# Two-block transformer kernel in fp32: the last four weight units of two projections used tile by tile

## The reference

```python
h = modulate(rms_norm(x, norm_g[0]), sh_m, sc_m)
y = stick_breaking_mixer(h, w_qkv, w_o)      # ends in o @ w_o, 1024 x 1024
x = x + gt_m * rms_norm(y, norm_g[1])
h = modulate(rms_norm(x, norm_g[2]), sh_f, sc_f)
g, u = split(h @ w_in)                       # 1024 x 5632
y = (silu(g) * u) @ w_out                    # 2816 x 1024
x = x + gt_f * rms_norm(y, norm_g[3])
```

## Time and profile before

| | |
|---|---|
| time, median of 3 | 2371.11 us (2367.22 to 2376.46) |
| the profiled execution, its own time | 2365.49 us |
| its span, first to last instruction | 2363.7 us |
| busy PE, PEld, DVE, ACT, POOL | 1796.4, 1117.7, 1291.7, 868.9, 904.2 us |
| mean granted clock of PE | 0.83 |

### The profile page before, as it was taken

How to read it: one execution, slowest core, us unless ns; L and a number is a source line. 1 busy time by engine, 2 the same in 40 slices (tenths; PEclk the granted TensorE clock), 3 DMA queues, 4 the chain that set the end, 5 groups by cost and what they waited for, 6 DMA issues and landing times. The chain is left out here.

```text
span 2363.7 us, 25240 instructions
## 1 busy us (share of the span) xinstructions
PE 1796.4 (76%) x8848; PEld 1117.7 (47%) x8848; DVE 1291.7 (55%) x2801; ACT 868.9 (37%) x2355; POOL 904.2 (38%) x699
## 2 busy tenths in 40 slices
PE   8898899868777787564443468885377897999998
PEld 6775676445435255110000014331055676888786
DVE  4633668877787665656767676566403623333201
ACT  3122344333444343233643353333225734222212
POOL 1300334374663444344555544445400122444343
PEclk9999888777788889786555679986579998999999
DMA  6111999999999999999999999999953011122121
GB/s 246 54 63 49 403 410 392 418 377 411 411 401 418 418 418 417 417 404 406 419 420 420 419 405 419 418 397 419 420 178 110 1 72 71 72 107 107 72 107 54
DMA packets 108494, 687.78 MB, mean 291 GB/s; under 512 B 12240, under 2 KB 13264, under 8 KB 40144
## 3 DMA queue, kind: packets, MB, share of 16 engines
q0 software_dynamic: 73728, 536.90, 55.3%
q1 hardware_dynamic: 34640, 149.27, 16.9%
HBM read 681.40 MB, written 2.10 MB: 289 GB/s over the span
## 5 line engine op out<-in xcount | busy, mean ns | idle before, releaser
L747 PE MATMUL ps<-arena 128*32 128x512 f32 (+5 forms) x4376 | 872.7, 587 | 377.0 <-ACT arena L1452 337.3
L1696 POOL DMA_INDIRECT arena<-in_experts,arena_u x512 | 608.6, 1189 | 770.9 <-PE ps L747 678.2
L2001 DVE CUSTOM_DVE_ANT_0 arena<-arena 128x1024 f32<-128x1024 f32 x512 | 653.2, 1281 | 384.3 <-DMA arena<-in_experts,arena_u 367.5
L747 PEld LDWEIGHTS ps<-arena 128*128 128x128 f32 (+2 forms) x4376 | 443.2, 167 | 735.5 <-ACT arena L1452 496.6
L1448 ACT ACTIVATE sel<-sel 128x1 f32<-128x1 f32 x512 | 102.8, 201 | 705.4 <-DVE sel L2001 697.7
L1717 POOL TENSOR_TENSOR r_low<-middle,r_low 128x1024 fp32r<-128x1024 f32 x74 | 178.7, 2415 | 463.5 <-ACT r_low L1533 463.5
L747 PE MATMUL ps<-r_low 128*128 128x512 f32 x1248 | 286.4, 391 | 5.3 <-DVE r_low L2059 3.8
L747 PEld LDWEIGHTS ps<-r_low 128*128 128x128 f32 x1248 | 234.6, 189 | 56.8 <-DVE r_low L2059 4.4
L1452 ACT ACTIVATE arena<-arena,sel 128x32 f32<-128x32 f32 x512 | 164.5, 321 | 16.8 <-ACT sel L1448 0.2
L1533 ACT ACTIVATE r_low<-middle 128x1024 fp32r<-128x1024 f32 x74 | 78.3, 1058 | 208.1 <-PE ps L747 208.1
L747 PE MATMUL ps<-upper,arena 128*128 128x384 f32 (+5 forms) x640 | 144.9, 412 | 3.2 <-issue 3.0
(11 more groups left out here) (203 smaller groups left out, 1721.2 us busy)
## 6 DMA issues: line engine op xcount, KB each, us to landing
arena<-in_w_front SPq DMA_DIRECT2D x88, 512.0 KB, 3.5
middle<-in_w_late SPq DMA_DIRECT2D x18, 2048.0 KB, 8.2
arena<-in_w_qkv SPq DMA_DIRECT2D x48, 512.0 KB, 10.7
gtrow<-in_w_ada SPq DMA_DIRECT2D x32, 512.0 KB
arena<-in_experts,arena_u POOLq DMA_INDIRECT x512
arena<-in_w_ada SPq DMA_DIRECT2D x16, 512.0 KB, 10.0
x<-in_x SPq DMA_DIRECT2D x4, 512.0 KB, 8.7
arena<-in_sub_keys SPq DMA_DIRECT2D x2, 1024.0 KB, 10.4
```

Source lines behind the costliest of these rows:

```text
L747: return nc.tensor.matmul(out_, lhsT, rhs, start=start, stop=stop_, skip_group_check=skip)
L1696: nc.gpsimd.indirect_dma_start(ring[n % RING], None, a["experts"], bass.IndirectOffsetOnAxis(ap=idxq[:, i % 4, k:k + 1], axis=0),).then_in ...
L2001: nc.vector.tensor_tensor_reduce(r[:, 0:D], r[:, 0:D], xrep[k % 4], 1.0, 0.0, ALU.mult, ALU.add, dots[:, n % 8:n % 8 + 1]).then_inc(s["dot ...
```

## The change

Three things are changed in what each engine does.

- **Two groups of four units.** Units 4 to 7 and units 70 to 73 go through `split_last`: PE first waits for all four units' `u_lo`, then goes over the token tiles, and for each tile issues the 24 matmuls of the four units. `y` is told after each tile. The four units need four buffers: units 4 to 7 have buffers of their own in a region that the attention has left, units 70 and 71 keep the two of before, units 72 and 73 stand where `a_lo` was. `split_after` says how many units must have been used before ACT may write a unit: none for 4 to 7, 3 and 4 for units 8 and 9, 52 for units 72 and 73, and u-1 for all others (70 and 71 too). ACT splits the units in the same order as before, except that unit 9 now comes right after unit 8.
- **Transposes and modulation per tile.** After tile t's branch, PE transposes its own tile into that tile's two banks; tile 0's transposes stand between the matmuls of tiles 2 and 3, the others behind tile 3. ACT modulates a tile in eight instructions of 128 x 128 (four for tiles 2 and 3, where DVE does the other four), then copies the tile to `a_hi` in one instruction of 128 x 1024; DVE subtracts it in one. Unit 8 waits once for all four tiles of `a_lo`.
- **Places.** `tail` and `tail_sq` have a place of their own for k = 0, since the first tiles' tails now run while `a_hi` is still read. The attention's two swap semaphores (`qswap`, `kswap`) become one, `swap`, with the sum of the counts.

The diff, cut to its core:

```diff
-        u_hi = [low3(32 + 8 * n, KD, P) for n in range(2)]
-        u_lo = [low3(36 + 8 * n, KD, P) for n in range(2)]
+        u_hi = [low3(32 + 8 * (u % 2), KD, P) for u in range(UNITS)]
+        u_lo = [low3(36 + 8 * (u % 2), KD, P) for u in range(UNITS)]
+        for n, kb in enumerate((112, 120, 84, 92)):
+            u_hi[UNIT_O2 + 4 + n], u_lo[UNIT_O2 + 4 + n] = high3(kb, KD, P), high3(kb + 4, KD, P)
+        for n in range(2):
+            u_hi[UNITS - 2 + n], u_lo[UNITS - 2 + n] = low3(16 + 8 * n, KD, P), low3(20 + 8 * n, KD, P)
+        def split_after(u):
+            if UNIT_O2 + 4 <= u < UNIT_FIN:
+                return 0
+            if UNIT_FIN <= u < UNIT_FIN + 2:
+                return UNIT_O2 + 3 + u - UNIT_FIN
+            return UNIT_FOUT if u >= UNITS - 2 else u - 1
...
-        tail_sq, tail_sq2 = region(8, D), region(120, D)
+        tail_sq, tail_sq2 = [region(kb, D) for kb in (104, 8)], region(108, D)
...
             def split_tile(out_, u, k, rows_hi, rows_lo):
                 for kd in range(KD):
-                    if u == UNIT_FIN:
-                        pe.wait_ge(s["a_lo"], kd + 1)
-                    mm(out_, u_hi[u % 2][:, kd, :], rows_hi[:, kd, :], kd == 0, False)
-                    mm(out_, u_hi[u % 2][:, kd, :], rows_lo[:, kd, :], False, False)
-                    ins = mm(out_, u_lo[u % 2][:, kd, :], rows_hi[:, kd, :], False, kd == KD - 1)
+                    if u == UNIT_FIN and kd == 0:
+                        pe.wait_ge(s["a_lo"], T)
+                    mm(out_, u_hi[u][:, kd, :], rows_hi[:, kd, :], kd == 0, False)
+                    mm(out_, u_hi[u][:, kd, :], rows_lo[:, kd, :], False, False)
+                    ins = mm(out_, u_lo[u][:, kd, :], rows_hi[:, kd, :], False, kd == KD - 1)
                 return ins.then_inc(s["unit_used"], 1)
-            def split_rows(out_of, u, k_of, cols_hi, cols_lo, kts, first, last):
-
-
-                w_hi, w_lo = halves(u_hi[u % 2]), halves(u_lo[u % 2])
+            def split_tile_rows(t, u, k_of, cols_hi, cols_lo, last):
+                w_hi, w_lo = halves(u_hi[u]), halves(u_lo[u])
+                tok = slice(t * P, (t + 1) * P)
+                for hf in range(2):
+                    kt, n = k_of(u, hf)
+                    out_ = ps[:, 2 * t + n, :]
+                    mm(out_, cols_hi[:, kt, tok], w_hi[:, hf, :], kt == 0, False)
+                    mm(out_, cols_hi[:, kt, tok], w_lo[:, hf, :], False, False)
+                    ins = mm(out_, cols_lo[:, kt, tok], w_hi[:, hf, :], False, kt == last)
+                return ins
+            def split_rows(units, k_of, cols_hi, cols_lo, last):
+                for u in units:
+                    unit(u)
+                    for t in range(T):
+                        ins = split_tile_rows(t, u, k_of, cols_hi, cols_lo, last)
+                    ins.then_inc(s["unit_used"], 1)
+            def split_last(units, k_of, cols_hi, cols_lo, last, between):
+                for u in units:
+                    unit(u)
                 for t in range(T):
-                    tok = slice(t * P, (t + 1) * P)
-                    for hf in range(2):
-                        kt, n = k_of(hf)
-                        begin, end = kt == first, kt == last
-                        mm(out_of(t, n), cols_hi[:, kt, tok], w_hi[:, hf, :], begin, False)
-                        mm(out_of(t, n), cols_hi[:, kt, tok], w_lo[:, hf, :], False, False)
-                        ins = mm(out_of(t, n), cols_lo[:, kt, tok], w_hi[:, hf, :], False, end)
-                    if t < T - 1 and end and kts is not None:
-                        ins.then_inc(s[kts], 1)
-                return ins.then_inc(s["unit_used"], 1)
+                    for u in units:
+                        ins = split_tile_rows(t, u, k_of, cols_hi, cols_lo, last)
+                    if t < T - 1:
+                        ins.then_inc(s["y"], 1)
+                    between(t)
+                ins.then_inc(s["unit_used"], len(units))
+                pe.wait_ge(s["unit_used"], units[-1] + 1)
+                nc.tensor.nop().then_inc(s["y"], 1)
...
-            for t in range(T):
+            def rows_after(t):
+                pe.wait_ge(s["yfree"], t + 1)
                 pe.wait_ge(s["xs"], T + t + 1)
                 for kd in range(KD):
-                    ins = mm(ps[:, kd, t * P:(t + 1) * P], x[:, t, kd * P:(kd + 1) * P], tdiag[:, t, :])
+                    ins = mm(ps[:, 2 * t + kd // 4, kd % 4 * P:(kd % 4 + 1) * P], x[:, t, kd * P:(kd + 1) * P], tdiag[:, t, :])
                 ins.then_inc(s["tr"], 1)
+            def o_rows(u, hf):
+                return (u - UNIT_O2) % 4 * 2 + hf, (u - UNIT_O2) // 4
+            split_rows(range(UNIT_O2, UNIT_O2 + 4), o_rows, a_hi, a_lo, KD - 1)
+            split_last(range(UNIT_O2 + 4, UNIT_FIN), o_rows, a_hi, a_lo, KD - 1, lambda t: rows_after(0) if t == 2 else None)
+            for t in range(1, T):
+                rows_after(t)
             for j in range(FT):
                 if j >= 4:
                     pe.wait_ge(s["ffd"], j - 3)
@@ -1276,12 +1308,11 @@
                     unit(UNIT_FIN + 2 * j + n)
                     split_tile(ps[:, 2 * j % 8 + n, :], UNIT_FIN + 2 * j + n, 1, a_hi, a_lo)
             pe.wait_ge(s["ffd"], FT)
-            for kt in range(FT):
-                unit(UNIT_FOUT + kt)
-                split_rows(lambda t, n: ps[:, 2 * t + n, :], UNIT_FOUT + kt, lambda hf: (kt, hf),
-                           act_hi, act_lo, "y", 0, FT - 1)
-            pe.wait_ge(s["unit_used"], UNITS)
-            nc.tensor.nop().then_inc(s["y"], 1)
+            def fout_rows(u, hf):
+                return u - UNIT_FOUT, hf
+            split_rows(range(UNIT_FOUT, UNITS - 4), fout_rows, act_hi, act_lo, FT - 1)
+            split_last(range(UNITS - 4, UNITS), fout_rows, act_hi, act_lo, FT - 1, lambda t: None)
...
-                if u >= 2:
-                    sc.wait_ge(s["unit_used"], u - 1)
-                nc.scalar.activation(u_hi[u % 2], raw_unit(u), ACT.Copy).then_inc(s["u_hi"], 1)
-
-            def high(kd):
-
-                sc.wait_ge(s["a_y"], KD * T + kd + 1)
-                nc.scalar.activation(a_hi[:, kd, :], y_hT[:, kd, :], ACT.Copy).then_inc(s["a_hi"], 1)
+                if split_after(u) > 0:
+                    sc.wait_ge(s["unit_used"], split_after(u))
+                nc.scalar.activation(u_hi[u], raw_unit(u), ACT.Copy).then_inc(s["u_hi"], 1)
...
-            for u in range(UNIT_O2 + 2, UNIT_FIN + 1):
+            for u in range(UNIT_O2 + 2, UNIT_FIN + 2):
...
+            def rows_after(t):
+                at = slice(t * P, (t + 1) * P)
+                sc.wait_ge(s["tr"], T + t + 1)
+                for kd in range(KD if t < 2 else KD // 2):
+                    nc.scalar.activation(y_hT[:, kd, at], ps[:, 2 * t + kd // 4, kd % 4 * P:(kd % 4 + 1) * P], ACT.Identity,
+                                         bias=modc[:, 2, kd:kd + 1], scale=stat_mod(1, kd)).then_inc(s["a_y"], 1)
+                sc.wait_ge(s["a_y"], KD * T + (KD * (t + 1) if t < 2 else KD * 2 + KD // 2 * (t - 1)))
+                if t >= 2:
+                    sc.wait_ge(s["a_yd"], KD // 2 * (t - 1))
+                nc.scalar.activation(a_hi[:, :, at], y_hT[:, :, at], ACT.Copy).then_inc(s["a_hi"], 1)
+            for t in range(3):
+                branch(0, t)
+                stats_after(t)
+            rows_after(0)
+            branch(0, 3)
+            rows_after(1)
+            stats_after(3)
             nc.scalar.preload_act_table_set("silu_and_others")
-            split(UNIT_FIN + 1)
-            sc.wait_ge(s["tr"], 2 * T)
-            for kd in range(KD):
-                nc.scalar.activation(y_hT[:, kd, :], ps[:, kd, :], ACT.Identity, bias=modc[:, 2, kd:kd + 1],
-                                     scale=stat_mod(1, kd)).then_inc(s["a_y"], 1)
-                high(kd)
+            rows_after(2)
+            rows_after(3)
...
+            def rows_after(t):
+                ve.wait_ge(s["tr"], T + t + 1)
+                for kd in range(KD // 2, KD):
+                    ts(y_hT[:, kd, t * P:(t + 1) * P], ps[:, 2 * t + 1, (kd - 4) * P:(kd - 3) * P], stat_mod(1, kd), modc[:, 2, kd:kd + 1],
+                       ALU.mult, ALU.add).then_inc(s["a_yd"], 1)
+            def low(t):
+                at = slice(t * P, (t + 1) * P)
+                ve.wait_ge(s["a_hi"], t + 1)
+                tt(a_lo[:, :, at], y_hT[:, :, at], a_hi[:, :, at], ALU.subtract).then_inc(s["a_lo"], 1)
+            for t in range(3):
+                branch(0, t)
+                norm_after(t)
+            low(0)
+            branch(0, 3)
+            rows_after(2)
+            norm_after(3)
+            low(1)
+            low(2)
+            rows_after(3)
+            low(3)
```

More of the change, by code:

```diff
@@ L568, in block_kernel @@
         ff = middle3(80, 2, S)
-        tail = region3(0, 2, D)
+        tail = [region3(kb, 2, D) for kb in (132, 0)]
         s = {}
@@ L579, in block_kernel @@
```

(28 more changed lines are left out.)

12 lines of the change are left out of this document (removed).

## The result

| | before | after |
|---|---|---|
| time, median of 20 runs | 2372.1 us (2364.36 to 2379.01) | 2377.09 us (2371.06 to 2385.47) |
| ratio to before | | 1.0030 (95%: 1.0020 to 1.0041) |
| span of the profiled execution | 2363.7 us | 2383.4 us |
| mean granted clock | 0.830 | 0.828 |

The account below looks back on a forecast made before the run. PE was taken to bound the kernel nearly all of the way. The terms 8.5 + 2.1 - 3.8 + 0.4 = +7.2 us, added to the median of 2371.11 us, gave 2378.3 us (ratio 1.003), range 2368 to 2385.

Parts of the forecast that it names:

- The wait ahead of units 70 to 73: At unit 69's end PE idles 8.5 us until units 71 to 73 are copied and subtracted.
- The clock behind it: After the 8.5 us pause before the last 96 matmuls, half clock costs 2.1 us (bounds 1.6 and 2.6).
- a clock that stays low: Rival: the last tile-wise matmuls run at 1.2 GHz to the end, 10.9 us instead of 2.1, 2387 us; chance 0.09.
- The end's gain: After the last output projection three tails are hidden and one stands behind PE: 3.8 us gained.
- The wait ahead of units 4 to 7: In the output projection PE idles 2.5 us after unit 3 until unit 7's subtraction is done.
- Its clock: After the 2.5 us pause before unit 4, half clock costs 1.6 us (bounds 0 and 2.6).
- The middle: From tile 2's end to unit 8: unit 8 starts 25.5 us later, ends at 1992.8 us, a loss of 0.4 us.
- The hidden waits: Rival: ACT and POOL are further ahead, so both pauses and their clock losses fall away, 2363.6 us; chance 0.07.
- The middle gains: Rival: the tile chain before unit 8 overlaps better or the clock stays up, 4 to 5 us less, 2374; chance 0.13.
- The middle loses: Rival: before unit 8 small pieces cost more or a step is not hidden, 4 us more, 2382; chance 0.11.
- The sum: Whole kernel: 8.5 + 2.1 - 3.8 + 0.4 = +7.2 us, giving 2378.3 us, ratio 1.003; chance 0.60.

Follow-up runs that it names:

- e7_last_three: The changed kernel with three units (71 to 73) instead of four taken tile by tile at the end; ratio to before 1.0006.
- e3_last_two: The changed kernel with only the last two units (72 and 73) taken tile by tile at the end; ratio to before 0.9993.
- e2_end_only: The kernel before with only the last four units of the second FFN's output projection taken tile by tile; median 2379.61 us, ratio 1.0038.
- e6_filler: The changed kernel with nine added matmuls, their output overwritten, in PE's pause before unit 4; ratio to before 1.0006.
- e4_both: The changed kernel with only two units tile by tile at the end, and units 4 and 5 prepared before 2 and 3; ratio to before 0.9971.

## Why the prediction was right, point by point

- *The wait ahead of units 70 to 73.* Predicted 8.5 us of idle PE, measured 8.26: POOL's three subtractions on end took 6.94 us and not 7.3. They came 2.3 us apart, under the 2.40 of one alone, where I had put gaps of 0.05 between them; the row of four in 5.27 us could not show a gap. e7_last_three and e3_last_two show the mechanism.
- *The clock behind it.* Predicted 2.1 us. The 96 matmuls took 24.37 us against 4 x 5.44 = 21.8, 2.6 more, which is the upper bound. But 0.3 of this is not the clock's: 96 matmuls at full clock (units 0 to 3) also take 22.05 from first start to last end. So the clock lost 2.3. In e2_end_only the row was 24.26 and in e6_filler 24.14, 2.2 and 2.1. The rival of a clock that stays low did not occur: it was at full again from 2357 on (0.81 in 2356 to 2358).
- *The end's gain.* Predicted 3.8 us, measured 3.8 where nothing else is in the way (e3_last_two, 29.8 to 26.0). Together the last stretch was to lose 8.5 + 2.1 - 3.8 = 6.8, and lost 7.1.
- *The wait ahead of units 4 to 7.* Predicted 2.5, measured 2.24. Its clock, predicted 1.6 us and argued from the row of the 2.35 us pause, was 1.6 in the profiled execution of the changed kernel (18.22 against 16.62), and nothing in two others of the same code. A mean over the four is 0.8, half of what I took, so the sum is wrong by under a us. The rule of the Trainium skill ("TensorE: Matmul & The Clock Gate", the part on HAM oscillation in real kernels), weighed against the row, says that no such pause costs the clock. The two executions that stayed at 1.00 agree with it, the two that fell to 0.50 do not.
- *The middle.* Predicted: unit 8 starts 25.5 us behind tile 2's end. Tile 2's matmuls end at about 1971.75 after, unit 8 starts at 1996.61: 24.9. The pieces on DVE took 1.36 for four (1.4 taken), ACT's eight 2.81 to 2.89 (2.91 taken), tile 3's transposes 3.57 rather than 2.5. Unit 8 itself took 8.1 us where 7.5 were predicted. The stretch was to lose 0.4 us, and lost 0.4: the smaller pause and the shorter chain made up for the slower restarts, so part of this agreement is luck. So is the execution: in the two whose clock stayed up behind the first pause the stretch gained 0.9 and 1.1 us.
- *The rivals.* The hidden waits did not occur. "The middle gains" has one of its two reasons on its side, a clock that stays up, but only behind the first pause and in two of four executions, for 1.2 to 1.4 us and not 4 to 5. The 3.5 us of e4_both come from an order that the change does not have. "The middle loses" did not occur: the pieces took 0.34 to 0.38 us each.
- *The sum.* 7.2 us predicted, 7.5 by the stretches, 1.003 by the runs. The predicted 2378.3 us stands beside a median of 2377.09. That nearness is partly luck: the 2371.11 it started from was the median of three, the median of 20 is 2372.10, and the medians then differ by 5.0 and not 7.2; the interval of the ratio takes in both.

What I did not see is how near the gain was. I priced the wait for units 70 to 73 but did not ask which number of units PE has cover for: two need no wait at all, and keep all of the tails' gain.

## What to carry to other kernels

A group of units that is to be ready at once wants its preparation paid in advance: compare what the preparing engines need for the group from the moment its first buffer is free with the work that the consumer still has beside it, and take the largest group that this covers (here 8.3 us of preparation, so two units, 10.9 us of cover). A pause of the matmul engine on the path costs its length and, behind all of 4.6 us and more here and some of 2.2, a restart at half clock, so order the preparation by when the group needs it, not by number. And where single executions vary by more than the effect, compare stretches of the trace between the same two instructions, in more than one execution where the clock can fall either way (here 1.6 us).

## What the runs showed of the hardware

- A pause of PE of 2.23 or 2.24 us was followed by half clock in two profiled executions (72 matmuls in 18.22 us) and by no drop in two others of the same code (16.62), one of 2.92 us by none (16.61). A pause of 2.35 us was followed by a granted clock of 0.50 in both executions that have it, before and e2_end_only. From unit 0 on, every pause of 4.57 us or more in the ten profiles was followed by half clock. The pause of 8.26 us was followed by 2.1 to 2.3 us of loss in all three that have it (24.14 to 24.37 us for 96 matmuls against 22.05 at full clock).
- Discarded matmuls in a pause buy back the half clock: 14 of them within 6.3 us took unit 8 from 8.5 to 5.7 us (one execution each; without them it took 7.2 to 8.5 us in seven).
- Executions of one kernel differ by 6 to 25 us. In the two profiles of before and after, 12.0 of the 19.7 us arise ahead of unit 0, 10.1 of them by the last expert gather (1701.4 and 1711.5 us); what sets this is open.
